# Two transformer blocks in one launch on one core: the 32x32-block turn keeps both token tiles of a 32-token group side by side

## What is computed

```python
mkv  = rmsnorm(mem, g_mem) @ w_mem_kv
proj = rmsnorm(x, g_in) @ w_in                      # q, k, v, z of the branches, and three gates
merged = sigmoid(g_a) * (ya @ w_proj_a) + sigmoid(g_b) * (yb @ w_proj_b) + sigmoid(g_m) * (ym @ w_proj_m)
x = rmsnorm(x + merged @ w_out, g_final)
h = x + concat(y_lru, y_ret) @ w_out_2              # both made from rmsnorm(x) @ w_in_2
u = rmsnorm(h, ln2)
h = h + (silu(u @ w_gate) * (u @ w_up)) @ w_down
out = rmsnorm(h, g_final_2)
```

## Time and profile before

| what | before |
|---|---|
| median of 3 runs | 2201.22 us (2200.91 to 2202.69) |
| the profiled execution | 2200.99 us |
| its span, first to last instruction | 2199.2 us |
| PE busy | 2183.5 us (99%) |
| DVE busy | 1303.1 us (59%) |
| ACT busy | 1027.7 us (47%) |
| DMA, mean | 211 GB/s |

### The profile page before, as it was taken

The page is one execution under the profiler, slowest core; times in us unless marked ns, Lnnn a source line. Parts: engine busy times, 40 slices in busy tenths (PEclk is TensorE's granted clock), DMA queues, the critical chain, the costliest instruction groups (busy, mean ns, idle before and its releaser), DMA issues.

```text
span 2199.2 us, 26113 instructions
## 1 busy us (share of the span) xinstructions
PE 2183.5 (99%) x9906; PEld 1810.7 (82%) x9906; DVE 1303.1 (59%) x1559; ACT 1027.7 (47%) x1235; POOL 144.6 (7%) x242
## 2 busy tenths in 40 slices
PE   8999999999999999999999999999999999999998
PEld 7888888888888888888888888888888888888886
DVE  5755656676455645546676888665555555554544
ACT  5544444444444444444555666454444444444443
POOL 0010101011000000000111100110001000100000
PEclk9999999999999999999999999999999999999999
DMA  8775656577754657667778756676777777776664
GB/s 290 220 231 174 204 170 211 183 227 233 211 160 151 213 179 227 202 207 280 231 255 253 227 185 192 199 246 207 216 213 224 216 211 215 229 227 199 194 195 145
DMA packets 228674, 464.65 MB, mean 211 GB/s; under 512 B 16345, under 2 KB 16609, under 8 KB 227681
## 3 DMA queue, kind: packets, MB, share of 16 engines
q1 hardware_dynamic: 212128, 408.73, 59.4%
q0 software_dynamic: 15712, 53.49, 8.0%
q10 hardware_dynamic: 736, 1.12, 0.1%
HBM read 437.59 MB, written 25.69 MB: 211 GB/s over the span
## 4 chain that ended last, share of the span: by engine, by line
PE 95%; DMA 2%; DVE 2%; issue 1%; ACT 1%; POOL 0%; SPq 0%; POOLq 0%; ACTq 0%; DVEq 0%
PE ps L1483 30%; PE ps L1485 30%; PE ps L1484 30%; DMA stage<-bounce 1%; PE ps L1374 1%; PE ps L1396 1%; PE ps L1343 1%; DVE w_lo L864 1%; DMA bounce<-tmp 0%; DMA raw<-in_w_mem_kv 0%; PE ps L1385 0%; ACT w_hi L578 0%; DVE tmp L1025 0%; POOL stage L521 0%; DVE stage L1020 0%
## 5 line engine op out<-in xcount | busy, mean ns | idle before, releaser
L864 DVE TENSOR_TENSOR w_lo<-raw,w_hi 128x1024 fp32r<-128x1024 f32 (+1 forms) x776 | 931.6, 1211 | 765.3 <-ACT w_hi L578 764.2
L578 ACT ACTIVATE w_hi<-raw 128x1024 fp32r<-128x1024 f32 (+1 forms) x776 | 811.6, 1052 | 912.3 <-PE ps L1485 826.0
L1483 PE MATMUL ps<-w_hi,xT_hi 128*128 128x512 f32 x1088 | 430.1, 395 | 0.4 <-DVE w_lo L864 0.4
L1485 PE MATMUL ps<-w_hi,xT_lo 128*128 128x512 f32 x1088 | 424.2, 390 | 0.0
L1484 PE MATMUL ps<-w_lo,xT_hi 128*128 128x512 f32 x1088 | 423.6, 389 | 0.0
L1483 PE MATMUL ps<-w_hi,u2T_hi 128*128 128x512 f32 x704 | 274.0, 389 | 0.0
L1485 PE MATMUL ps<-w_hi,u2T_lo 128*128 128x512 f32 x704 | 273.9, 389 | 0.0
L1484 PE MATMUL ps<-w_lo,u2T_hi 128*128 128x512 f32 x704 | 273.9, 389 | 0.0
L1485 PEld LDWEIGHTS ps<-w_hi,xT_lo 128*128 128x128 f32 x1088 | 204.2, 188 | 43.2
L1483 PEld LDWEIGHTS ps<-w_hi,xT_hi 128*128 128x128 f32 x1088 | 204.4, 188 | 42.5 <-DVE w_lo L864 1.9
L1484 PEld LDWEIGHTS ps<-w_lo,xT_hi 128*128 128x128 f32 x1088 | 204.5, 188 | 41.0
(11 more groups left out here) (262 smaller groups left out, 2250.0 us busy)
## 6 DMA issues: line engine op xcount, KB each, us to landing
raw<-in_w_in SPq DMA_DIRECT2D x368, 512.0 KB, 4.4
raw<-in_w_ffn_gate SPq DMA_DIRECT2D x88, 512.0 KB, 4.3
raw<-in_w_ffn_up SPq DMA_DIRECT2D x88, 512.0 KB, 4.5
raw<-in_w_ffn_down SPq DMA_DIRECT2D x88, 512.0 KB, 4.6
raw<-in_w_out SPq DMA_DIRECT2D x64, 512.0 KB, 5.1
bounce<-tmp POOLq DMA_DIRECT2D x41, 512.0 KB, 3.3
stage<-bounce POOLq DMA_DIRECT2D x164, 128.0 KB, 5.3
raw<-in_w_mem_kv SPq DMA_DIRECT2D x32, 512.0 KB, 5.9
```

The source lines that it names most:

```text
L578: nc.scalar.activation(w_hi[:, s, 0:per], raw[:, s, 0:per], ACT.Copy).then_inc(hi_ready, 1)
L864: nc.vector.tensor_tensor(w_lo[:, s, 0:per], raw[:, s, 0:per], w_hi[:, s, 0:per].bitcast(F32), ALU.subtract)\
L1483: nc.tensor.matmul(bank(2 * par + t), x_hi, w_hi[:, s, k], start=first, stop=False)
L1485: ins = nc.tensor.matmul(bank(2 * par + t), x_lo, w_hi[:, s, k], start=False, stop=last)
```

## The change

The element order of the turned blocks changes. Before, `tmp` held for each token tile t the columns (m, c, a), so that the two token tiles of one 32-token group lay 2 KB apart in a row of `bounce`, and a read took eight pieces of 512 bytes for each partition. Now `tmp` holds (m, t, c, b): both token tiles stand side by side, and a read takes four pieces of 1 KB. With this order a copy out of `stage` has one dimension too many for a single instruction over both token tiles. ACT's copy of four column groups is made in two instructions, one for each token tile. DVE's low part is made in two instructions of 128x512 instead of four of 128x256, and for the residual tiles in eight of 128x128 instead of four of 128x256. The factor of one half leaves these instructions: for the feed-forward product it goes into `square` (DVE, once per norm), and for the merged branches into the residual add. The bytes moved and the number of DMAs stay.

```diff
-        turned = stage[:, :, :].rearrange("p t (q c b) -> p c (t q) b", c=QUAD, b=32)
+        turned = stage[:, :, :].rearrange("p t n -> p (t n)").rearrange("p (q t c b) -> p c t q b", q=4, t=NT, c=QUAD)
+        blocks_of = tmp[:, :, :].rearrange("p t n -> p (t n)").rearrange("p (m t c b) -> p t m c b", m=4, t=NT, c=QUAD)
...
-                        pool.dma_start(stage[32 * m:32 * (m + 1), :, :].rearrange("p t (q x) -> p t q x", q=4),
-                                       bounce.rearrange("(q a) (t m x) -> m a t q x", a=32, t=NT, m=4)[m]).then_inc(b_in, 16)
+                        pool.dma_start(stage[32 * m:32 * (m + 1), :, :].rearrange("p t n -> p (t n)").rearrange("p (q x) -> p q x", q=4),
+                                       bounce.rearrange("(q a) (m x) -> m a q x", a=32, m=4)[m]).then_inc(b_in, 16)
...
-                        nc.scalar.activation(by_block(dst[:, bass.ds(kind[-1] * QUAD, QUAD)]), turned, ACT.Copy, scale=0.5)\
-                          .then_inc(b_hi, 1)
+                        to = by_block(dst[:, bass.ds(kind[-1] * QUAD, QUAD)])
+                        for t in range(NT):
+                            ins = nc.scalar.activation(to[:, :, t], turned[:, :, t], ACT.Copy)
+                        ins.then_inc(b_hi, 1)
...
-                ins = nc.vector.tensor_tensor(f["square"], f["r"], f["r"], ALU.mult)
+                ins = nc.vector.scalar_tensor_tensor(f["square"], f["r"], 0.5, f["r"], ALU.mult, ALU.mult)
...
-                    ins = nc.vector.transpose(tmp[:, t], src(t).rearrange("p (c m a) -> p m c a", c=4, m=4))
+                    ins = nc.vector.transpose(blocks_of[:, t], src(t).rearrange("p (c m a) -> p m c a", c=4, m=4))
...
-                    last = nc.vector.tensor_tensor(dst[:, :, cs], dst[:, :, cs], both(par), ALU.add)
+                    last = nc.vector.scalar_tensor_tensor(dst[:, :, cs], both(par), 0.5 if what == "u" else 1.0, dst[:, :, cs], ALU.mult, ALU.add)
...
-                            ins = nc.vector.scalar_tensor_tensor(lo, turned[:, k], cols[:, f["v"] + kc:f["v"] + kc + 1], hi,
-                                                                 ALU.mult, ALU.subtract)
+                            for t in range(NT):
+                                ins = nc.vector.scalar_tensor_tensor(lo[:, t], turned[:, k, t], cols[:, f["v"] + kc:f["v"] + kc + 1], hi[:, t],
+                                                                     ALU.mult, ALU.subtract)
...
-                        for k in range(QUAD):
-                            ins = nc.vector.scalar_tensor_tensor(lo[:, k], turned[:, k], 0.5, hi[:, k], ALU.mult, ALU.subtract)
+                        for t in range(NT):
+                            ins = nc.vector.tensor_tensor(lo[:, :, t], turned[:, :, t], hi[:, :, t], ALU.subtract)
```

More of the change, by code:

```diff
@@ L236, in by_block @@
         def by_block(ap):
-            return ap.rearrange("p c (u b) -> p c u b", b=32)
+            return ap.rearrange("p c (t q b) -> p c t q b", t=NT, b=32)
         ps = ctx.enter_context(nc.psum_tensor("ps", [P, 8 * NW], F32))
@@ L707, in post_job @@
                     src = ps[:, 4 * NW:6 * NW].rearrange("p (c s) -> p c s", s=S)
-                    nc.scalar.activation(mrgT_hi[:, bass.ds(kind[-1] * QUAD, QUAD)], src, ACT.Copy, scale=0.5).then_inc(tx_hi[0], 1)
+                    nc.scalar.activation(mrgT_hi[:, bass.ds(kind[-1] * QUAD, QUAD)], src, ACT.Copy).then_inc(tx_hi[0], 1)
                 w.count_job(prev)
@@ L723, in use_late @@
                             kc = kind[2] * QUAD + c
-                            ins = nc.scalar.activation(hi[:, kc].rearrange("p (u b) -> p u b", b=32), turned[:, c], ACT.Copy,
+                            ins = nc.scalar.activation(hi[:, kc].rearrange("p (t q b) -> p t q b", t=NT, b=32), turned[:, c], ACT.Copy,
                                                        scale=cols[:, v + kc:v + kc + 1])
@@ L728, in use_late @@
                         dst = ffT_hi if kind[0] == "ffu" else mrgT_hi
-                        nc.scalar.activation(by_block(dst[:, bass.ds(kind[-1] * QUAD, QUAD)]), turned, ACT.Copy, scale=0.5)\
-                          .then_inc(b_hi, 1)
-                    else:
-                        nc.scalar.activation(by_block(kind[1][:, kind[2]:kind[2] + QUAD]), turned, ACT.Copy).then_inc(b_used, 1)
+                        to = by_block(dst[:, bass.ds(kind[-1] * QUAD, QUAD)])
+                        for t in range(NT):
+                            ins = nc.scalar.activation(to[:, :, t], turned[:, :, t], ACT.Copy)
+                        ins.then_inc(b_hi, 1)
+                    else:
+                        to = by_block(kind[1][:, kind[2]:kind[2] + QUAD])
+                        for t in range(NT):
+                            ins = nc.scalar.activation(to[:, :, t], turned[:, :, t], ACT.Copy)
+                        ins.then_inc(b_used, 1)
                     w.step("b")
@@ L1120, in post_job @@
                     dve.wait_ge(tx_hi[0], w("h0", 1))
-                    nc.vector.scalar_tensor_tensor(mrgT_lo[:, c], ps[:, 4 * NW:6 * NW].rearrange("p (c s) -> p c s", s=S), 0.5,
-                                                   mrgT_hi[:, c].bitcast(F32), ALU.mult, ALU.subtract).then_inc(tx_free[0], 1)
+                    nc.vector.tensor_tensor(mrgT_lo[:, c], ps[:, 4 * NW:6 * NW].rearrange("p (c s) -> p c s", s=S),
+                                            mrgT_hi[:, c].bitcast(F32), ALU.subtract).then_inc(tx_free[0], 1)
                 w.count_job(prev)
@@ L1137, in use_late @@
                             kc = kind[2] * QUAD + k
-                            lo, hi = (m[:, kc].rearrange("p (u b) -> p u b", b=32) for m in (f["lo"], f["hi"].bitcast(F32)))
-                            ins = nc.vector.scalar_tensor_tensor(lo, turned[:, k], cols[:, f["v"] + kc:f["v"] + kc + 1], hi,
-                                                                 ALU.mult, ALU.subtract)
+                            lo, hi = (m[:, kc].rearrange("p (t q b) -> p t q b", t=NT, b=32) for m in (f["lo"], f["hi"].bitcast(F32)))
+                            for t in range(NT):
+                                ins = nc.vector.scalar_tensor_tensor(lo[:, t], turned[:, k, t], cols[:, f["v"] + kc:f["v"] + kc + 1], hi[:, t],
+                                                                     ALU.mult, ALU.subtract)
                         ins.then_inc(b_used, 1)
```

## The result

| what | before | after |
|---|---|---|
| median | 2201.73 us (2200.91 to 2204.63, 8 runs) | 2206.9 us (2205.53 to 2210.01, 8 runs) |
| ratio, with its 95% interval | | 1.0024 [1.0013, 1.0035] |
| the profiled execution | 2200.99 us | 2205.66 us |
| its span | 2199.2 us | 2203.9 us |
| last output landed | 2198.78 us | 2199.76 us |

What follows compares the result with a forecast made beforehand. PE's own work was taken as the bound. -0.5 us at 520 and 542 and +0.8 us at 1088 gave +0.3 us on the profiled 2200.99 us, 2201.3 us; the median 0.2 us above, 2201.5 us; range 2199.8 to 2203.3 us.

Steps and rivals of the forecast that it cites:

- the time is PE's own work, and that the other engines count only where they make PE wait: Between first and last product PE idles only 1.6 us, so changes on DVE, ACT or transfers are mostly swallowed.
- Nothing else that the change touches makes PE wait: Only the late products near 520 and 542 us and at 1088 us, behind turned blocks, were counted as PE waits.
- The low parts: DVE's eight 128x128 for residual tiles take 2.2 us, 0.5 us more each; two before the 1088 stall add 0.8 us.
- given back by the earlier read: In the `w_out` tiles, a read landing sooner offsets 0.2 us of the first longer low part's 0.5 us.
- The stalls at 520 and 542: Three carries, each 0.2 us shorter, remove PE's losses of 0.15 and 0.45 us; counted as -0.5 us.
- turns at 690 ns: DVE's turns, now writing four runs of 128 elements instead of one of 512, keep their 690 ns: no cost.
- the fourth rival: DVE's turns with strided output take up to twice as long ahead of PE's splits: 2208.5 us; 5%.
- copies in pairs of 1.15 us: ACT's copy out of `stage`, split into two of 128x512, takes 1.16 us, 0.1 us more than the single one.
- factors for nothing: Moving the factor of one half into DVE's `square` and residual add costs nothing; the add reads the same operands.
- 0.2 us less in issuing four reads: POOL issues 128 pieces a read instead of 256, 0.06 us less each; the fourth read goes out 0.2 us sooner.
- no wait of PE in the feed-forward tiles: DVE's larger low parts there save 0.05 to 0.15 us, counted as nothing; a wait appearing there would refute the prediction.
- the third rival: Reads land as before and copies cost 0.2 us: +0.6 us at 542, +1.05 us at 1088, 2202.9 us; 19%.

Runs made afterwards that it cites:

- with one, three and six small DMAs: Changed kernel with one, three or six DMAs of 1024 pieces of 64 bytes added on POOL behind the first carry: 1.0014, 1.0015, 1.0017.
- old order in 18 to 20: Changed kernel with the three residual blocks of `w_out` written, read, copied and made low as before: 2205.39 us against 2202.07, 1.0015.
- old order in 29 and 30: Changed kernel with the two residual blocks of `w_out_2` (for `u2`) written, read, copied and made low as before: 2203.74 us against 2202.07, 1.0009.
- before with small low parts: Kernel before, with the residual tiles' low part in eight instructions of 128x128 instead of four of 128x256: 2203.15 us against 2202.73, 1.0005.
- with three and with one small DMA: Kernel before with DMAs added on POOL behind the first carry: three (1024, 128 and 128 pieces) 0.9998; one of 512 pieces 1.0002.
- old order in five tiles, without and with small DMAs: Changed kernel with residual blocks 18 to 20, 29 and 30 handled as before: 1.0002; with three DMAs of 1024 64-byte pieces added on POOL: 1.0003.
- the repeat: The changed kernel measured once more, unaltered: 2207.72 us against 2201.99, 1.0026.
- POOL's early end: Last norm's roots moved from POOL to ACT and DVE: changed kernel 2202.73 us, 1.0003; before 2201.79, 0.9997; changed with five residual tiles as before 2202.0, 1.0001.

## Why the prediction was wrong

**The step that failed.** It is the sentence that "the time is PE's own work, and that the other engines count only where they make PE wait": the sum counted only PE's waits between its products, and put nothing, without a reason, for what follows the last one. POOL's closing drain stood in the trace of before, with 6.45 us and 0.1 us of margin to the last landing, and no row of the prediction shows it; the change leaves POOL's instructions and their order alone. The changed reads made it 9.96 us. That is 3.7 us of the 4.7 us, and the edit that takes the drain out of the way gives 4.2 us back, 0.4 us of it by quicker roots. With it out of the way the time is 2202.73 us, inside the range that was given. "Nothing else that the change touches makes PE wait" failed too, at 1111 us (below).

How the drain goes with the time, over all kernels that were timed with POOL's program ending last:

| drain | pause at block 20 | kernels | ratio to before |
|---|---|---|---|
| 9.96 us | yes | changed; again | 1.0024, 1.0026 |
| 9.96 us | no | with one, three and six small DMAs; old order in 18 to 20 | 1.0014, 1.0015, 1.0017, 1.0015 |
| 6.45 us | yes | old order in 29 and 30 | 1.0009 |
| 6.45 us | no | before with small low parts, with three and with one small DMA; old order in five tiles, without and with small DMAs | 1.0005, 0.9998, 1.0002, 1.0002, 1.0003 |

The means over each length are 1.00185 and 1.0003; their difference, 0.00155 of 2202 us, is 3.4 us, where the drains differ by 3.5 us. Taken with the pause alone or without it alone the difference is 0.0016 and 0.0013. The pause at block 20 would then be worth 0.0007 to 0.0010, 1.5 to 2.2 us, more than the profiles show at 1111 us; single ratios are known to 0.0009 only, so this size stays open.

**The low parts: right mechanism, too small a size.** Eight of 128x128 take 2.19 us, as worked out (2.2). Added at 1088 were to be 0.8 us, since 0.2 us of the first part would be given back by the earlier read. The distance near 1088 was 0.43, 0.49 and 0.43 us in three kernels with large low parts and no pause there (none to be seen in a fourth), and 1.87, 1.07, 1.21, 1.59, 2.39, 1.28, 1.98 and 1.05 us in eight with small ones and the changed reads, 1.55 us in the mean: 1.1 us more. With the old reads it was 1.4 us more in one profile. That one is the only kernel in which the low parts alone differ: none had large low parts and the changed reads without a pause at block 19, and the four with such a pause have 0.72 to 2.09 us. So the 1.1 us isn't shown to be the low parts' alone, and no run shows that the earlier read gives anything back. In the profile of after it had landed at 1077.98, 1.9 us ahead of its use at 1079.86; what held ACT was the weight load, for which it waited 4.32 us until 1077.20. That this load comes later because DVE frees its slot later, behind the first low part, is argued and wasn't measured.

**A pause of POOL, not foreseen.** With 2.43 us from a turn to its write at 1090.17, and 2.0 us more until that write had landed, it put 1.3 us on PE at 1111 in the profile of after, 0.5 us in the repeat and 0.7 us in the kernel with POOL's early end, whose program is the same up to there. The kernel before has a pause too, 1.9 us at block 14; the changed reads moved it to another block.

**The stalls at 520 and 542.** They were to vanish, -0.5 us. In the profile of after no product comes more than 0.31 us after its forerunner from 541 to 545 us, and the copies are as priced:

```profile
530.86 1.15 ACT L737 ACTIVATE kbT<-stage 128x512 f32<-128x512 f32 x2 [4.21 <-DMA stage<-bounce]
531.92 2.94 ACT L579 ACTIVATE w_hi<-raw 128x1024 fp32r<-128x1024 f32 x3
```

But the same program in other profiles lost more there than before: from 500 to 563 us the repeat lost 0.3 us more, and the version with POOL's early end 2.7 us more (their POOL programs are the same up to there). From 478 to 563 us the twelve profiles with 1 KB reads there lost between -0.5 and 2.9 us more than the profile of before, 0.9 us in the mean; the five with 512 byte reads (before itself counted as 0) lost 0.8 us in the mean. So no run shows the -0.5 us of the sum, nor any gain from the 1 KB pieces. That a read lands as before agrees with the rule that the prediction cited (the Trainium skill, DMA: Bandwidth & Descriptors, Specifications: from 512 bytes on a transfer runs at line rate); the median went from 5.3 to 5.2 us.

**Right as they stood:** turns at 690 ns (the fourth rival, priced at 2208.5 us, came near the measured time with a mechanism that isn't there), copies in pairs of 1.15 us, factors for nothing, 0.2 us less in issuing four reads, no wait of PE in the feed-forward tiles. The chance of 6 in 100 for slower was held for the turns and a little for waits that the third rival makes elsewhere.

## What stays open

Why the drain is 9.96 or 6.45 us, and why POOL pauses. It is none of: the number of small DMAs added (one to six left it), the number of pieces (with the period that fitted, above), or how late the drain starts (the short one started from 2192.2 to 2199.0 us, the long one from 2193.3 to 2195.6 us). In every kernel seen, the long one goes with the new order in the blocks 29 and 30, the short one with the old order there; those two were only changed together and no other late block was tried alone. POOL's last pause differs as well: the four kernels with the new order in the late blocks but the old one in 29 and 30 have one of 1.0 us among the reads of the last block, 41, and no other kernel has. Moving the drain to 1967 us also left a difference: it then ended 4.5 us after the last read had landed in the changed kernel, and 2.75 us after in the two others.

## What to carry to other kernels

When PE is busy from end to end, look also at what closes the launch: the last output's landing, each engine's closing drain, and the margin between them. An engine with a long closing drain and nothing left to do should end its program early; here that put the drain behind PE's work and took away nearly all that the changed reads cost (1.0024 to 1.0003). It gains nothing that shows where the drain ends ahead of the last landing, as in the kernel before. Small instructions right ahead of a split that PE waits for can cost more than their own sum: two groups, each 0.5 us longer, stood in the chain of a stall that grew by 1.1 us in the mean.

## What the runs showed of the hardware that was not expected

- POOL's closing drain takes one of two lengths, 6.45 us (within 3 ns over seven kernels) or 9.96 us (within 3 ns over seven profiles of six kernels), though its queue's last read had landed over 200 us before.
- POOL pauses at fixed places of a program, the same in every profile of it: 1.9 us between a landing and the first read in the kernel before (block 14, and again in both variants whose POOL program is the same there), 2.43 us ahead of the write of block 20 in the changed kernel, 2.3 us ahead of block 21's when one, two, three or six small DMAs are added, 2.42 us ahead of the reads of block 19 in three kernels with the old order in 18 to 20 and 1.5 us among them in the fourth. (The 2.3 and 2.4 us are counted from the release; 0.3 us is the usual.) Others are 0.1 to 1.0 us. The trace shows nothing that POOL waits for. A write behind such a pause took longer to land: 5.3 to 6.4 us at block 20 (3.3 us in the kernels without), 6.0 to 6.9 us at block 21 (3.3 to 4.6 us without).
- The number and size of the pieces of POOL's reads went with both (the pause from block 14 to 20, the drain from 6.45 to 9.96 us). The small DMAs moved the pause by one block and left the drain.
